# Layer-0 modulation by column blocks: ScalarE and VectorE copies, TensorE products, three projection tiles at once

## The chip, the core and the metric

The kernel runs on one NeuronCore of a Trainium2 chip. The metric is the device time of one execution in microseconds (us), first instruction to last, with the small overhead around it. The engines are TensorE (PE; its weight loads are shown as PEld), VectorE (DVE), ScalarE (ACT), GpSimd (POOL) and SyncE (SP), whose queue starts nearly all transfers. The profile also gives the clock granted to TensorE, as a share of 2.4 GHz; its two levels are 1.2 and 2.4 GHz (0.50 and 1.00).

## The reference

A network of several mixer layers in float32 on 1024 tokens of width 1024. Only the entry of the first layer matters here:

```python
c_act = jax.nn.silu(c)
mod = c_act @ ada_w[layer] + ada_b[layer]            # 1024 -> 3072
shift, scale, gate = jnp.split(mod, 3, axis=-1)
h = rms_norm(x, norm_w[layer]) * (1.0 + scale) + shift
... = even_mixer(h, even_w_in, ...)                   # begins with h @ even_w_in
```

For the first layer, shift and scale are the first 2048 columns of `mod`. They are needed before the first product with `even_w_in`. The gate is needed much later and is computed elsewhere, as before.

## The kernel before

Features lie on the partitions: `X` is eight feature tiles of 128 features by 1024 tokens. Every engine's instructions are written by hand in program order, and engines meet through semaphores only (`signal(...)`, `.up`, `.landed`, `.at`). An engine whose next instruction waits holds back everything behind it, and this is true of SP's queue of transfers too.

**The start.** `sp_start` loads the identity, `x` in two transfers of 2 MB (`XIN`, tokens on partitions), 20 small rows of parameters (`PACKA`, `PACKB`), then the first 2048 columns of `ada_w` as eight blocks of 128 rows (`AWK`, 1 MB each, four buffers). TensorE turns the parameter rows into columns and transposes `x` by feature tiles (`pe_start`, 8 transposes of 128x128 for each tile); ScalarE copies every tile from PSUM to `X` and squares `XIN` for the norm. VectorE multiplies each row block by its entry of silu(c) and adds it up in `ACK` (`dve_row_block`, 2048 columns). When all eight blocks are in, TensorE sums `ACK` over partitions by 16 products with a column of ones (line 598), and VectorE makes `MOD` (shift, scale) and `GS` (the gain). `pe_stay_awake(n, bank)` multiplies the identity n times with a result nobody reads.

**The modulation.** `dve_scaled` multiplies X by the spread reciprocal roots (`XN`); `act_modulate` and `dve_modulate` make `T1 = XN*GS + MOD`, ScalarE rounds it to `HH` and VectorE subtracts to get the rest `HL` (`n_low`), one feature tile after another.

**The projection.** `EVEN_PROJ` is a list of output tiles j = 0, 1, 2, ... of 128 columns of `even_w_in`. A tile's weights are loaded to `WR` by `sp_weights`, rounded to `WH` by ScalarE (`act_high`), and the rest goes to `WL` by GpSimd (`pool_low`). There are two sets of these buffers, for even and odd tiles. `pe_feature` issues six matmuls of 128x512 for one feature k of a tile (WH with HH, WH with HL, WL with HH, each on two halves of the tokens). Tiles 0 and 1 run side by side (`pe_two_tiles`), since they must keep pace with the making of `HL`. Tile 2 and the others follow one by one. Tiles 0 to 2 are the latents; each is copied and squared by ScalarE (`act_latent`) and its squares are summed by TensorE with eight products of one column (`pe_latent_sums`, line 818). Tile 3 is `EVEN_V`, tile 4 `EVEN_KR` (32 columns, `stacked`: four matmuls a feature).

**SP's order around it.** After the row blocks come the weights of tiles 0, 1 and 2 (tile 2's when `WL` of tile 0 is made), the spill of `X`, then, once `n_low` of the last feature is there, five tables for the rotations (COSA, SINA, BLK, COSB, SINB), and only then the weights of tile 3:

```python
for j, t in enumerate(EVEN_PROJ):
    if 0 < j < len(EVEN_PROJ) - 2:
        sp_weights(t + 2)
    if j == 0:
        sp.wait_ge(*ack_summed.at(1))
        sp.wait_ge(*n_low.at(0, DT - 1))
        ... tables ...
```

Of the kernel before, what the change touches and what calls it, by code (L numbers as in the profile page):

```python
# [122 lines left out]
def build(nc, d, where, known):  # L123
# [81 lines left out]

    def places(t):
# [9 lines left out]
    w_loaded = [signal("w_loaded0"), signal("w_loaded1")]  # L216
    w_high, w_low, w_used = signal("w_high"), signal("w_low"), signal("w_used")
# [4 lines left out]

    def sp_weights(t):
        if t >= 2:
            sp.wait_ge(*w_low.at(t - 2))
        raw, _, _ = places(t)
        for dst, src in tiles[t].pieces(raw):
            sp.dma_start(dst, src).then_inc(*w_loaded[t % 2].landed(t))

    def act_high(t):  # L230
        raw, high, _ = places(t)
        user = t - 2
        while user >= 0 and tiles[user].own:
            user -= 2
        act.wait_ge(*w_loaded[t % 2].at(t))
# [9 lines left out]
    def pe_feature(t, k, high, low):  # L245
        s, w = t % 2, tiles[t]
        _, wh, wl = places(t)
        if k == 0:
            pe.wait_ge(*w_low.at(t))
            if t >= 2:  # L250
                pe.wait_ge(*evicted(t - 2))
        both = WH[:, s, 0:w.kt, 0:w.out]
        terms = ((both, high), (both, low)) if w.stacked else ((wh, high), (wh, low), (wl, high))
        for n, (wt, x) in enumerate(terms):
            for h in range(2):
                last = pe.matmul(ps[0:w.out, 2 * s + h, :], wt[:, k, :], x[:, k, halves(h)],  # L256
# [30 lines left out]

    def act_evict(t, dst, func=ACT.Copy, scale=1.0):
# [4 lines left out]
    EVEN_LAT = [tile(cols(even_in, E_CQ + i * P)) for i in range(3)]  # L293
# [190 lines left out]
    AWK, ACK = place("AWK", 79.5, [P, 4, 2 * DM]), place("ACK", 145.5, [P, 2 * DM])  # L484
    XN = place("XN", 175.5, [P, DT, SEQ])
    MKW, MKA = place("MKW", 3, [P, 2, DM]), place("MKA", 11, [P, DM])
    PACKA, PACKB = place("PACKA", 143.5, [P, P]), place("PACKB", 144, [P, P])
# [22 lines left out]
    x_in = [signal("x_in0"), signal("x_in1")]  # L510
    awk_loaded = [signal(f"awk_loaded{i}") for i in range(4)]
    act_scaled = signal("act_scaled")
    awk_used, ack_summed, sums_made, xn_made = signal("awk_used"), signal("ack_summed"), signal("sums_made"), signal("xn_made")
    packs_clear, packs_turned, cols_copied, cs_made = (signal("packs_clear"), signal("packs_turned"), signal("cols_copied"),
                                                       signal("cs_made"))
    x_turned, x_copied, x_spilled, x_back = signal("x_turned"), signal("x_copied"), signal("x_spilled"), signal("x_back")
# [46 lines left out]

    def sp_start():
        sp.dma_start(IDENT[:, :], const("ident")).then_inc(*ident_in.landed())
        for i in range(2):
            sp.dma_start(XIN[:, 4 * i:4 * i + 4, :], d["x"][0].rearrange("(t p) n -> p t n", p=P)[:, 4 * i:4 * i + 4, :]).then_inc(
                *x_in[i].landed())
        sp.wait_ge(*packs_clear.at())
        for i, (dst, src) in enumerate(packs):  # L570
            sp.dma_start(dst, src).then_inc(*packs_in.landed(i))
        for k in range(DT):
            if k >= 4:
                sp.wait_ge(*awk_used.at(k - 4))
            sp.dma_start(AWK[:, k % 4, :], d["ada_w"][0, rows(k), 0:2 * DM]).then_inc(*awk_loaded[k % 4].landed(k))

    def pe_start():
        pe.wait_ge(*ident_in.at())
        pe.wait_ge(*packs_in.at(len(packs) - 1))
        pe.transpose(ps[:, 4, 0:P], PACKA[:, :], IDENT[:, :])  # L580
        pe.transpose(ps[:, 4, P:2 * P], PACKB[:, :], IDENT[:, :]).then_inc(*packs_turned.up())
        for i in range(2):
            pe.wait_ge(*x_in[i].at())
        for f in range(DT):
            if f >= 2:
                pe.wait_ge(*x_copied.at(f - 2))
            for t in range(TT):
                last = pe.transpose(pair(2 * (f % 2))[:, rows(t)], XIN[:, t, rows(f)], IDENT[:, :])
            last.then_inc(*x_turned.up(f))
            if f == 3:  # L590
                pe_spread(0)
        pe.wait_ge(*cols_copied.at())
        pe.wait_ge(*x_copied.at(DT - 1))
        pe_stay_awake(10, 0)
        for half in range(2):
            pe.wait_ge(*awk_used.at(DT - 1, half))
            for m in range(8 * half, 8 * half + 8):
                last = pe.matmul(ps[:, 4, m:m + 1], ACK[:, rows(m)], ONEC[:, 0:1], start=True, stop=True)
            last.then_inc(*ack_summed.up(half))
        pe_stay_awake(20, 0)  # L600

    def act_start():
        for t in range(TT):
            act.wait_ge(*x_in[t // 4].at())
            if t >= 2:
                act.wait_ge(*sums_made.at(t - 2))
            act.activation(SQX[:, t % 2, :], XIN[:, t, :], ACT.Square, accum_out=S1[:, t:t + 1]).then_inc(*sums_made.up(t))
            if t == 2:
                act.wait_ge(*cols_copied.at())
                act.activation(CS[:, :], col["c"], ACT.Silu).then_inc(*cs_made.up())  # L610
        act_root(0)
        for f in range(DT):
            act.wait_ge(*x_turned.at(f))
            act.activation(X[:, f, :], pair(2 * (f % 2)), ACT.Copy).then_inc(*x_copied.up(f))

    def dve_row_block(k):

        dve.wait_ge(*awk_loaded[k % 4].at(k))
        if k:
            dve.wait_ge(*awk_used.at(k - 1))  # L620
        w, c = AWK[:, k % 4, :], CS[:, k:k + 1]
        if k == 0:
            dve.tensor_scalar(ACK[:, :], w, c, None, ALU.mult).then_inc(*awk_used.up(k))
        elif k < DT - 1:
# [3039 lines left out]
```

## Time and profile before

| | us |
|---|---|
| runs, median (lowest to highest of 3) | 2331.66 (2328.37 to 2333.32) |
| profiled execution, its time | 2328.58 |
| profiled execution, its span | 2327.3 |
| granted clock over the span | 0.993 |
| TensorE busy | 2258.5, 97% of the span |
| first matmul of the projection | at 53.25 |
| first matmul of tile 3 | at 91.84 |
| first matmul of tile 4 | at 104.57 |

Times of rows count from the start of the span. A row of the timeline gives start, duration, engine, line, operation, output<-input, count, and in brackets the idle time before it with its releaser. A TensorE product in float32 is recorded as two (a transpose as one), so "x16" for a line of 128x1 products is eight instructions. The last matmul of a row is drawn until it has drained, so rows of TensorE overlap a little; pace is read from start to start.

### The profile page before, as it was taken

To read this page: it belongs to the slowest core of one execution; us is meant where nothing else is said; L and a number is where in the kernel's file an instruction comes from. 1 tells how busy PE (TensorE), PEld (TensorE's weight loads), DVE (VectorE), ACT (ScalarE), POOL (GpSimd) and SP (SyncE) were. 2 spreads that over 40 slices of the span, in tenths; PEclk is the share of its full clock that TensorE was granted. 3 is DMA by queue.
4 is the path that set the end of the run, shared out by engine and by line. 5 is a ranking of instruction groups with operands and counts; after the bars stand their busy time and mean duration, and the time that the engine had idled before them with its cause. 6 is when DMAs were issued, how large, how long until landed. Compare 5 with 4: busy or idle time off the path is not lost.

```text
span 2327.3 us, 29639 instructions
## 1 busy us (share of the span) xinstructions
PE 2258.5 (97%) x11342; PEld 1795.0 (77%) x11342; DVE 1410.2 (61%) x1784; ACT 1045.0 (45%) x1644; POOL 985.5 (42%) x674
## 2 busy tenths in 40 slices
PE   5999999999999999999999999999999999999998
PEld 5888755478888888866688677888878888888887
DVE  6256678668885275268845663442876666666665
ACT  5323265488883264357734562222333333333334
POOL 1111188546652138853122121122365555665551
PEclk9999999999999999999999999999999999999999
DMA  8255300010003133220031311132111111111111
GB/s 318 78 154 161 118 1 5 5 34 1 1 1 118 37 130 109 73 73 11 34 103 43 126 37 37 37 118 64 28 54 55 55 55 55 54 46 47 55 55 73
DMA packets 156385, 154.74 MB, mean 66 GB/s; under 512 B 12550, under 2 KB 141620, under 8 KB 154324
## 3 DMA queue, kind: packets, MB, share of 16 engines
q1 hardware_dynamic: 156244, 152.84, 21.1%
q8 instruction: 91, 1.49, 0.3%
q14 instruction: 50, 0.41, 0.1%
HBM read 128.05 MB, written 20.97 MB: 64 GB/s over the span
## 4 chain that ended last, share of the span: by engine, by line
PE 84%; ACT 5%; DVE 4%; issue 3%; POOL 2%; DMA 1%; SPq 0%; ACTq 0%; DVEq 0%; POOLq 0%
PE ps L256 29%; PE ps L3219 15%; PE ps L3236 9%; PE ps L1946 6%; PE ps L1366 3%; PE ps L1377 2%; PE ps L1165 2%; PE ps L2256 2%; PE ps L2239 2%; PE ps L2225 2%; PE ps L1188 2%; PE ps L1175 1%; PE ps L1348 1%; POOL WSL L3136 1%; ACT B_PR L1249 1%
## 5 line engine op out<-in xcount | busy, mean ns | idle before, releaser
L243 POOL TENSOR_TENSOR WL<-WR,WH 128x1024 fp32r<-128x1024 f32 (+2 forms) x71 | 163.9, 2309 | 656.2 <-ACT WH L238 656.0
L256 PE MATMUL ps<-HH,WH 128*128 128x512 f32 (+2 forms) x880 | 279.8, 399 | 0.4 <-issue 0.3
L256 PE MATMUL ps<-HL,WH 128*128 128x512 f32 (+2 forms) x880 | 273.6, 392 | 0.0
L256 PE MATMUL ps<-HH,WL 128*128 128x512 f32 x848 | 263.2, 392 | 0.0
L3449 DVE TENSOR_TENSOR XF<-ps,XF 128x1024 f32<-128x1024 f32 x168 | 201.6, 1220 | 32.5 <-PE ps L3236 25.9
L3219 PE MATMUL ps<-HC,WSH 128*128 128x512 f32 x640 | 197.1, 389 | 0.0
L256 PEld LDWEIGHTS ps<-HL,WH 128*128 128x128 f32 (+2 forms) x880 | 164.0, 186 | 37.7
L256 PEld LDWEIGHTS ps<-HH,WH 128*128 128x128 f32 (+2 forms) x880 | 160.2, 187 | 38.1 <-issue 5.3
L256 PEld LDWEIGHTS ps<-HH,WL 128*128 128x128 f32 x848 | 160.5, 189 | 34.2
L3136 POOL TENSOR_TENSOR WSL<-WSR,WSH 128x512 fp32r<-128x512 f32 x100 | 131.4, 1314 | 107.5 <-ACT WSH L3130 107.5
L3130 ACT ACTIVATE WSH<-WSR 128x512 fp32r<-128x512 f32 x100 | 62.9, 629 | 218.2 <-POOL WSR L3118 218.2
L3118 POOL TENSOR_TENSOR WSR<-WS 128x512 f32<-128x512 f32 x100 | 133.9, 1339 | 34.4 <-PE ps L3219 34.4
L3219 PE MATMUL ps<-HS,WSH 128*128 128x512 f32 x480 | 147.8, 389 | 0.0
L3219 PEld LDWEIGHTS ps<-HC,WSH 128*128 128x128 f32 x640 | 120.1, 188 | 25.0
L3219 PE MATMUL ps<-HC,WSL 128*128 128x512 f32 x320 | 124.5, 389 | 0.0
L3136 POOL TENSOR_TENSOR WSL<-WS,WSH 128x512 fp32r<-128x512 f32 x48 | 64.7, 1352 | 127.5 <-ACT WSH L3130 127.5
L3236 PE MATMUL ps<-AH,OWH 128*128 128x512 f32 x352 | 109.8, 393 | 6.4 <-DVE XF L3449 4.5
L3408 DVE TENSOR_TENSOR CG<-CG,ps 128x512 f32<-128x512 f32 x60 | 41.3, 688 | 119.1 <-ACT CG L3297 89.4
L3236 PE MATMUL ps<-AH,OWL 128*128 128x512 f32 x352 | 108.6, 390 | 0.0
L3236 PE MATMUL ps<-AL,OWH 128*128 128x512 f32 x352 | 108.5, 389 | 0.0
L238 ACT ACTIVATE WH<-WR 128x1024 fp32r<-128x1024 f32 (+2 forms) x73 | 68.5, 939 | 87.4 <-PE ps L256 72.8
L3219 PEld LDWEIGHTS ps<-HS,WSH 128*128 128x128 f32 x480 | 90.1, 188 | 18.7
(460 smaller groups left out, 5309.6 us busy)
## 6 DMA issues: line engine op xcount, KB each, us to landing
WS<-in_w_ffn_in SPq DMA_DIRECT2D x44, 512.0 KB, 5.1
MKW<-in_ada_w SPq DMA_DIRECT2D x32, 512.0 KB, 4.1
spill<-X SPq DMA_DIRECT2D x3, 4096.0 KB, 13.9
OW<-in_w_ffn_out SPq DMA_DIRECT2D x22, 512.0 KB, 3.6
WR<-in_w_in SPq DMA_DIRECT2D x19, 512.0 KB, 3.8
WR<-in_even_w_in SPq DMA_DIRECT2D x17, 512.0 KB, 4.1
AWK<-in_ada_w SPq DMA_DIRECT2D x8, 1024.0 KB, 9.3
X<-spill SPq DMA_DIRECT2D x2, 4096.0 KB, 13.6
```

The source lines that it names most:

```text
L238: act.activation(high[:, :, :], raw[:, :, :], ACT.Copy).then_inc(*w_high.up(t))
L243: pool.tensor_tensor(low[:, :, :], raw[:, :, :], high[:, :, :].bitcast(F32), ALU.subtract).then_inc(*w_low.up(t))
L256: last = pe.matmul(ps[0:w.out, 2 * s + h, :], wt[:, k, :], x[:, k, halves(h)], start=(k == 0 and n == 0), stop=(k == w.kt - 1 and n == len ...
L1165: last = pe.matmul(ps[:, b + j, :], qs[:, rows(q)], ks[:, halves(j)], start=(n == 0), stop=(n == len(passes) - 1))
L1366: last = pe.matmul(ps[:, e, :], keys[:, rows(k)], q[:, halves(u % 2)], start=(n == 0), stop=shifted)
L1946: last = pe.matmul(ps[:, bank, :], w[q % ORING][:, k, :], x[:, k, :], start=(k == 0 and m == 0), stop=(k == DT // 2 - 1 and m == 2))
L3118: pool.tensor_tensor(WSR[:, q % RING, :, :], w_block(*a), w_block(*b), op).then_inc(*ws_sum.up(q))
L3130: act.activation(WSH[:, q % RING, :, :], src, ACT.Copy).then_inc(*ws_high.up(q))
L3136: pool.tensor_tensor(WSL[:, q % RING, :, :], src, WSH[:, q % RING, :, :].bitcast(F32), ALU.subtract).then_inc(*ws_low.up(q))
L3219: last = pe.matmul(ps[:, BANK[o], :], w[:, q % RING, k, :], OPERAND[o][:, x, k, :], start=(k == 0 and n == 0), stop=(k == HK - 1 and n == 2))
L3236: done = pe.matmul(ps[:, 4 + 2 * (n % 2) + h, :], w[:, rows(n)], x[:, halves(h)], start=(first and m == 0), stop=(last and m == 2))
L3449: dve.tensor_tensor(LAST.x[:, n, :], pair(4 + 2 * (n % 2)), LAST.x[:, n, :], ALU.add).then_inc(*y_added.up(r, n))
```

## The change

It rewrites the start and the first three projection tiles.

- `x` comes in four transfers. Only `PACKA` is turned at the start; `PACKB` is loaded later and turned within the projection (`pe_packs`).
- `ada_w` comes by blocks of columns, `sp_mod_columns(f)`: for feature tile f, 128 shift and 128 scale columns of all 1024 rows (`AWC`, two transfers of 512 KB, four buffers). The block f needs the place of the block f-4.
- `pe_mod_columns(f)` makes shift and scale of feature tile f by 2 x 8 products of 128x1 with `CS` = silu(c), accumulated in PSUM. `BY_PE` is 8, so this holds for all eight tiles; `dve_mod_sum`, the way over VectorE, is issued for none.
- VectorE copies six of the eight tiles of X from PSUM, ScalarE two. The spread roots are copied to `RCS`. One VectorE instruction makes `T1 = X*GS*RCS`, ScalarE adds the shift while rounding to `HH`, and VectorE's `dve_lower` makes `HL`; `XN` is gone.
- `pe_three_tiles` runs tiles 0, 1 and 2 side by side; tile 2 has its own buffers (`LAT_THIRD`) and PSUM banks 4 and 5. Before feature k it issues the products for tile k+2.
- The sums of all three latents come after tile 3.
- SP waits for the end of tile 2 (`w_used`) before the tables, since BLK lies where tile 2's rest weights are.

```diff
+    def pe_three_tiles(high, low, made, before):
+        ts = range(3)
+        for k in range(DT - 1):
+            before(k)
+            pe.wait_ge(*made(k))
+            for t in ts:
+                pe_feature(t, k, high, low)
+        before(DT - 1)
+        pe.wait_ge(*made(DT - 1))
+        for t in (1, 0, 2):
+            pe_feature(t, DT - 1, high, low)
...
+    BY_PE, BY_ACT = 8, (3, 5)
...
+    def sp_mod_columns(f):
+        if f < 4:
+            sp.wait_ge(*awk_loaded[f].at("x", f))
+        else:
+            sp.wait_ge(*ack_summed.at(f - 4))
+        for part in range(2):
+            src = d["ada_w"][0, :, part * DM + f * P:part * DM + (f + 1) * P].rearrange("(k p) n -> p k n", p=P)
+            sp.dma_start(AWC[:, f % 4, :, rows(part)], src).then_inc(*awk_loaded[f % 4].landed(f, part))
...
+            for part in range(2):
+                for k in range(DT):
+                    last = pe.matmul(ps[:, 6 + f % 2, 2 * f + part:2 * f + part + 1], AWC[:, f % 4, k, rows(part)], CS[:, k:k + 1],
+                                     start=(k == 0), stop=(k == DT - 1))
...
     def pe_start():
         pe.wait_ge(*ident_in.at())
+        pe_start_turn(0)
+        pe_start_turn(1)
+        pe.wait_ge(*packs_in.at(len(rows_a) - 1))
+        pe.transpose(ps[:, 6, 0:P], PACKA[:, :], IDENT[:, :]).then_inc(*packs_turned.up("a"))
+        for f in range(2, 5):
+            pe_start_turn(f)
+        pe.wait_ge(*cols_copied.at("a"))
+        pe_spread(0, spot=RC_SPOT)
+        for f in range(5, DT):
+            pe_start_turn(f)
+        for f in range(DT):
+            pe.wait_ge(*x_copied(f))
+        pe_mod_columns(0)
+        pe_stay_awake(10, 0)
+        pe_mod_columns(1)
+        pe_stay_awake(10, 0)
...
+        dve.scalar_tensor_tensor(T1[:, f % 2, :], X[:, f, :], GS[:, 0, f:f + 1], RCS[:, :], ALU.mult, ALU.mult).then_inc(
+            *n_scaled.up(0, f))
...
             if j == 0:
-                sp.wait_ge(*ack_summed.at(1))
                 sp.wait_ge(*n_low.at(0, DT - 1))
+                sp.wait_ge(*w_used.at(2))
                 for i, (dst, n) in enumerate(((COSA, "cosA"), (SINA, "sinA"), (BLK, "blk64"), (COSB, "cosB"), (SINB, "sinB"))):
...
-        pe_two_tiles(EVEN_PROJ[0], EVEN_PROJ[1], HH, HL, lambda k: n_low.at(0, k))
+        def before(k):
+            for f in {0: (2,), DT - 1: ()}.get(k, (k + 2,)):
+                if f < DT:
+                    pe_mod_columns(f)
+            if k == DT - 1:
+                pe_packs()
+
+        pe_three_tiles(HH, HL, lambda k: n_low.at(0, k), before)
         for j, t in enumerate(EVEN_PROJ):
-            if j > 1:
+            if j > 2:
                 pe_tile(t, HH, HL, beside=lambda k: beside(j, k))
-            if 1 <= j < 4:
-                pe_latent_sums(j - 1)
+            if j == 3:
+                pe.wait_ge(*ev_act.at(EVEN_LAT[2]))
+                for c in range(3):
+                    pe_latent_sums(c)
...
     def act_even_proj():
-        act_two_tiles(EVEN_PROJ[0])
         act_modulate()
         act.wait_ge(*qk_gains.at())
+        act_high(3)
+        act.wait_ge(*x_spilled.at(0))
+        for c in (1, 0, 2):
+            act_latent(c)
```

**SP's queue between the spill of X and the weights of tile 4** (`spill`, the five tables, then `WR` of tile 3 and of tile 4), before:

```order
L744 DMA spill<-X 128x8192 [waits x_copied]
L752 DMA COSA<-in_consts 128x1024 [waits n_low,ack_summed]
L752 DMA SINA<-in_consts 128x1024
L752 DMA BLK<-in_consts 128x128
L752 DMA COSB<-in_consts 128x1024
L752 DMA SINB<-in_consts 128x1024
L228 DMA WR<-in_even_w_in 128x8x128 [waits w_low]
L228 DMA WR<-in_even_w_in 128x8x32 [waits w_low]
```

The same place in SP's queue after the change:

```order
L817 DMA spill<-X 128x8192 [waits x_copied_dve,x_copied_act]
L825 DMA COSA<-in_consts 128x1024 [waits w_used,n_low]
L825 DMA SINA<-in_consts 128x1024
L825 DMA BLK<-in_consts 128x128
L825 DMA COSB<-in_consts 128x1024
L825 DMA SINB<-in_consts 128x1024
L235 DMA WR<-in_even_w_in 128x8x128 [waits w_low]
L235 DMA WR<-in_even_w_in 128x8x32 [waits w_low]
```

The order is the same; the first table now waits for `w_used`, which tile 2's last matmul raises, and the tables and both weight loads stand behind it.

**TensorE at the start of the projection**, before (`n_low` is HL of a feature made; the products of line 598 give shift and scale of all tiles):

```order
L598 MATMUL ps<-ONEC,ACK 128x1 [waits awk_used]
L598 MATMUL ps<-ONEC,ACK 128x1 x7
L374 MATMUL ps<-IDENT 128x128 x20
L256 MATMUL ps<-HH,WH 128x512 [waits w_low,n_low]
L256 MATMUL ps<-HH,WH 128x512
L256 MATMUL ps<-HL,WH 128x512 x2
L256 MATMUL ps<-HH,WL 128x512 x2
L256 MATMUL ps<-HH,WH 128x512 [waits w_low]
```

TensorE after the change, from tile 2's part of feature 0 (its weights are in `LAT_THIRD`) to the first matmuls of feature 1:

```order
L263 MATMUL ps<-HH,LAT_THIRD_88 128x512 [waits w_low]
L263 MATMUL ps<-HH,LAT_THIRD_88 128x512
L263 MATMUL ps<-HL,LAT_THIRD_88 128x512 x2
L263 MATMUL ps<-HH,LAT_THIRD_89 128x512 x2
L645 MATMUL ps<-CS,AWC 128x1 [waits awk_loaded3,mod_made]
L645 MATMUL ps<-CS,AWC 128x1 x15
L263 MATMUL ps<-HH,WH 128x512 [waits n_low]
L263 MATMUL ps<-HH,WH 128x512
```

A block of 16 products of 128x1 now stands ahead of each of the features 0 to 5, each followed by 18 matmuls of 128x512.

## Rows read from the trace of the kernel before

**Rows 1.** The page: span, busy time of engines, and the chain's shares.
```profile
span 2327.3 us, 29639 instructions
PE 2258.5 (97%) x11342; PEld 1795.0 (77%) x11342; DVE 1410.2 (61%) x1784; ACT 1045.0 (45%) x1644; POOL 985.5 (42%) x674
PE 84%; ACT 5%; DVE 4%; issue 3%; POOL 2%; DMA 1%; SPq 0%; ACTq 0%; DVEq 0%; POOLq 0%
```
**Rows 2.** The chain in order of time, 0 to 160 us: start, duration, what.
```profile
39.09 4.58 DVE ACK L629 x2
43.72 3.30 PE ps L598 x16
47.02 6.47 PE ps L374 x40
53.49 19.07 PE ps L256 x84
...
90.16 1.68 PE ps L818 x16
91.84 11.05 PE ps L256 x48
102.89 1.68 PE ps L818 x16
104.57 7.42 PE ps L256 x32
```
**Rows 3.** Line 567, the two transfers of x: starts, and time to landing.
```profile
L567 SPq DMA_DIRECT2D XIN<-in_x x2: 423/465/507, 1.2 to 1.7; - x2
DMA to landing us min/median/max: 8.0/10.4/12.8
```
**Rows 4.** The timeline of TensorE, 14 to 56 us.
```profile
17.56 0.45 PE L580 MATMUL ps<-IDENT,PACKA 128*128 128x128 f32 x1 [17.56 <-DMA PACKB<-in_a_k_norm]
...
18.01 3.62 PE L588 MATMUL ps<-IDENT,XIN 128*128 128x128 f32 x16
...
30.06 1.20 PE L406 MATMUL ps<-IDENT,SQX 128*128 128x128 f32 x8
31.10 1.91 PE L588 MATMUL ps<-IDENT,XIN 128*128 128x128 f32 x16
...
36.47 2.47 PE L374 MATMUL ps<-IDENT 128*128 128x128 f32 x20 [1.21 <-ACT X L614]
```
**Rows 5.** Groups by line and form, 0 to 400 us: busy, mean ns, idle.
```profile
L988 DVE COPY VA<-ps 128x1024 f32<-128x1024 f32 x1 | 1.2, 1225 | 0.8 <-PE ps L865 0.8
```
**Rows 6.** Stretches: busy of each engine, PEclk (third from the end), DMA, GB/s.
```profile
40.00:45.00 5.00, 3.23 (x24) 3.15 (x24) 4.80 (x3) 0.84 (x1) 5.00 (x2) 0.90 0.18 32
45.00:50.00 5.00, 5.00 (x24) 5.00 (x25) 2.46 (x5) 2.50 (x3) 0.88 (x1) 0.50 1.16 466
50.00:55.00 5.00, 5.00 (x36) 4.71 (x35) 5.00 (x5) 3.05 (x3) 0.00 (x0) 0.91 1.02 439
...
75.00:80.00 5.00, 4.66 (x26) 3.89 (x25) 0.00 (x0) 3.33 (x4) 2.78 (x2) 0.82 0.22 41
80.00:85.00 5.00, 5.00 (x20) 4.06 (x19) 0.00 (x0) 0.00 (x0) 0.76 (x1) 0.84 0.39 105
...
1460.00:1465.00 5.00, 5.00 (x23) 4.62 (x22) 0.00 (x0) 0.00 (x0) 0.00 (x0) 0.56 0.00 0
1465.00:1470.00 5.00, 5.00 (x18) 4.02 (x17) 1.16 (x2) 0.00 (x0) 0.00 (x0) 0.76 0.00 0
```
**Rows 7.** The timeline of TensorE, 1450 to 1472 us.
```profile
1457.63 1.92 PE L2648 MATMUL ps<-ONEC,OS 128*128 128x1 f32 x16 [0.60 <-DVE MIX L2899]
1459.41 0.71 PE L256 MATMUL ps<-HH,WH 128*128 128x512 f32 x2
...
1461.13 3.41 PE L2648 MATMUL ps<-ONEC,OS 128*128 128x1 f32 x16
```
**Rows 8.** The timeline, 66 to 112 us: tables, and tile 3's weights.
```profile
66.42 0.34 SPq L752 DMA_DIRECT2D COSA<-in_consts  x1
...
68.71 39.06 SPq L228 DMA_DIRECT2D WR<-in_even_w_in  x5
...
77.25 1.08 ACT L238 ACTIVATE WH<-WR 128x1024 fp32r<-128x1024 f32 x1
78.40 2.36 POOL L243 TENSOR_TENSOR WL<-WR,WH 128x1024 fp32r<-128x1024 f32 x1 [2.22 <-ACT WH L238]
```
**Rows 9.** Transfers issued 66 to 70 us: count, size, us to landing.
```profile
WR<-in_even_w_in SPq DMA_DIRECT2D x1, 512.0 KB, 7.4
```

More of the change, by code:

```diff
@@ L255, in pe_feature @@
             for h in range(2):
-                last = pe.matmul(ps[0:w.out, 2 * s + h, :], wt[:, k, :], x[:, k, halves(h)],
+                last = pe.matmul(ps[0:w.out, bank_of(t) + h, :], wt[:, k, :], x[:, k, halves(h)],
                                  start=(k == 0 and n == 0), stop=(k == w.kt - 1 and n == len(terms) - 1))
@@ L292, in build @@
     even_in, odd_in, second_in = d["even_w_in"][0], d["odd_w_in"][0], d["w_in_2"][0]
-    EVEN_LAT = [tile(cols(even_in, E_CQ + i * P)) for i in range(3)]
+    LAT_THIRD = own_places("LAT_THIRD", 35, 39, 43)
+    EVEN_LAT = [tile(cols(even_in, E_CQ + i * P), own=LAT_THIRD if i == 2 else None) for i in range(3)]
     EVEN_V = tile(cols(even_in, E_V))
@@ L564, in sp_start @@
     def sp_start():
         sp.dma_start(IDENT[:, :], const("ident")).then_inc(*ident_in.landed())
[L566 to L575, printed above, removed]
+        for i in range(4):
+            sp.dma_start(XIN[:, 2 * i:2 * i + 2, :], d["x"][0].rearrange("(t p) n -> p t n", p=P)[:, 2 * i:2 * i + 2, :]).then_inc(
+                *awk_loaded[i].landed("x", i))
@@ new lines, in sp_start, with pe_start_turn @@
+        sp.wait_ge(*packs_clear.at("a"))
+        sp_pack(0)
+        for t in range(3):
+            sp_weights(t)
+            sp_mod_columns(t)
+        sp_mod_columns(3)
+        sp.wait_ge(*packs_clear.at("b"))
+        sp_pack(1)
+        for f in range(4, DT):
+            sp_mod_columns(f)
+    def pe_start_turn(f):
+        if f >= 3:
+            pe.wait_ge(*x_copied(f - 3))
+        for t in range(TT):
+            if f == 0 and t % 2 == 0:
+                pe.wait_ge(*awk_loaded[t // 2].at("x", t // 2))
+            last = pe.transpose(pair(2 * (f % 3))[:, rows(t)], XIN[:, t, rows(f)], IDENT[:, :])
+        last.then_inc(*x_turned.up(f))
@@ new lines, in pe_mod_columns @@
+    def pe_mod_columns(f):
+        if f >= 2:
+            pe.wait_ge(*mod_made.at(0, "sum", f - 2))
+        if f >= BY_PE:
+            pe.wait_ge(*awk_used.at(f, DT - 1))
+            for part in range(2):
+                last = pe.matmul(ps[:, 6 + f % 2, 2 * f + part:2 * f + part + 1], ACK[:, f % 2, rows(part)], ONEC[:, 0:1], start=True,
+                                 stop=True)
+        else:
+            if f == 0:
+                pe.wait_ge(*cs_made.at())
+                pe.wait_ge(*rcs_made.at())
+            pe.wait_ge(*awk_loaded[f % 4].at(f, 1))
+            for part in range(2):
+                for k in range(DT):
+                    last = pe.matmul(ps[:, 6 + f % 2, 2 * f + part:2 * f + part + 1], AWC[:, f % 4, k, rows(part)], CS[:, k:k + 1],
+                                     start=(k == 0), stop=(k == DT - 1))
+        last.then_inc(*ack_summed.up(f))
@@ L577, in pe_start @@
     def pe_start():
         pe.wait_ge(*ident_in.at())
-        pe.wait_ge(*packs_in.at(len(packs) - 1))
[L580 to L600, printed above, removed]
+        pe_start_turn(0)
+        pe_start_turn(1)
+        pe.wait_ge(*packs_in.at(len(rows_a) - 1))
@@ new lines, in pe_start, with pe_packs @@
+        pe.transpose(ps[:, 6, 0:P], PACKA[:, :], IDENT[:, :]).then_inc(*packs_turned.up("a"))
[11 more added lines that the diff above has]
+        pe_stay_awake(10, 0)
+    def pe_packs():
+        pe.wait_ge(*mod_made.at(0, "sum", DT - 1))
+        pe.wait_ge(*packs_in.at(len(packs) - 1))
+        pe.transpose(ps[:, 7, 0:P], PACKB[:, :], IDENT[:, :]).then_inc(*packs_turned.up("b"))
@@ L661, in dve_start @@
[L661 to L680 removed]
+        dve_lower(0)
@@ L739, in sp_even_proj @@
     def sp_even_proj():
-        sp_weights(EVEN_PROJ[0])
-        sp_weights(EVEN_PROJ[1])
-        sp_weights(EVEN_PROJ[2])
-        sp.wait_ge(*x_copied.at(DT - 1))
+        for f in range(DT):
+            sp.wait_ge(*x_copied(f))
         sp.dma_start(d["spill"], X[:, :, :]).then_inc(*x_spilled.landed(0))
```

191 lines of the change are left out of this document (99 added, 92 removed).

## The prediction

> **What bounds the kernel now.** I read the page first: TensorE is busy 97% of the span of 2327.3 us and carries 84% of the chain that ended last [rows 1]. So a change to the start is worth what it moves TensorE's later work, and little behind it can give time back. Next, the chain in order of time [rows 2]. From 39.09 it runs over the last row block on VectorE (ending 43.7), the sums of 128x1 on TensorE, then the stay-awake matmuls into the first projection matmul at 53.5. From there on it is TensorE: tiles 0, 1, 2, one set of latent sums at 90.16, tile 3 at 91.84, a second set at 102.89, tile 4 at 104.57. I take the start of tile 4 as the mark, because from there both kernels issue the same work in the same order, and ask where the mark lies after the change.
>
> **When the start is over (PE free for the first block).** Its second half of x is issued at 1.7 and lands 12.8 later, so at 14.5 [rows 3]; four transfers bring the same bytes, so I keep 14.5 for the last. Tile 0 then lacks two transposes, tile 1 has eight. Sixteen took 3.4 us (3.62 with the drain) when TensorE had been idle, 0.21 each [rows 4]: 0.4 + 1.7 gives 16.6. PACKA stands behind x as the small rows did before, whose last landed at 17.4 to 17.5 [rows 4]. It may come as early as x, 14.5, but I take 17.4, the row it is nearest to. Turned at 17.6. Tiles 2, 3, 4 at 1.7 each: 22.7. The eight spread transposes ran in 1.04 start to start: 23.9 with its waits. Tiles 5, 6, 7 at the later pace of 0.12 each [rows 4], under 1.0 each: 26.7. VectorE copies tiles 6 and 7 from PSUM at 1.22 each, by a copy of this form [rows 5]: 28.4, and `pe_mod_columns(0)` waits for that. Bounds: 26 with early parameters, 31 if all transposes keep the slow pace. ScalarE's squares, roots and copies and the ada blocks of 1 MB lie beside this. The first of these blocks is issued right behind x, with one weight tile ahead of it, so it is there long before 28.4.
>
> The Trainium skill bears on the bound of 31: "TensorE: Matmul & The Clock Gate", Part 4 (PE-mode transpose), says that transposes do not count as work that raises the clock. The row at 31.10 speaks against it: 16 transposes in 1.91 us after the same took 3.62, with nothing but transposes between. By the page the sum would end about 3 us later, by the row where I put it.
>
> **The blocks of products (added).** The trace has no block of 16, but it has the same form in eights: weights of 128x128, one column. Eight took 1.68, so 0.21 each [rows 2], and 3.30 at the lower clock, 0.41 each [rows 2]. A block is 16, so 3.36 us at 2.4 GHz and 6.6 at 1.2. Eight blocks are 26.9 us of TensorE. Removed with them: the 16 sums of line 598 and 10 of the 30 stay-awakes, as well as VectorE's row blocks, all of them ahead of the old mark of 53.5 and already absent from the line above. Two blocks and two runs of ten stay-awakes (2.3 each without drain [rows 4]) come first: 28.4 + 6.7 + 4.6 = 39.7.
>
> **Three tiles with six blocks.** Tile 3 took 11.05 for 48 matmuls [rows 2], 1.38 for one feature. Three tiles are 24 x 1.38 = 33.1; the six blocks 20.2; PACKB's transpose 0.2. TensorE is never waited out by VectorE here: a feature costs TensorE 7.5 us, VectorE two instructions of about 1.2 and two of 0.2. End of the three tiles at a full clock: 93.2. Before, three tiles and one set of sums ended at 91.8.
>
> **The clock (added).** After eight products of one column the rows show the clock fall in places: from 78.2 to 81.6 (PEclk 0.82 in 75 to 80 and 0.84 in 80 to 85), 44 to 50.9 with sums of one column and a short idle at its start, and again near 1460 [rows 6]. That last place is the nearest to the new pattern: eight products, then six dense matmuls in 1.7 us, then eight products, which run at half pace, 3.41 us [rows 7], and some 6.4 us at 1.2 GHz in all (0.56 of one stretch, 0.76 of the next [rows 6]). The eights at 90.16 and 102.89, without idle before them and dense work on both sides, kept their pace of 1.68. The new blocks are twice that long and without a pause between products. So I expect a fall at each of the eight. A fall costs half its length: 1.7 us for one of 3.4, up to 3.3 for one of 6.4 to 6.9. Bounds are 0 (as at 90.16) and 8 x 3.3 = 26. I take eight short ones, 14, since every block from the third on is followed by 4.1 us of dense matmuls. End of the three tiles: 107.
>
> **Tile 3's weights (a wait moved).** SP now holds the tables, and behind them tile 3's weights, until tile 2's last matmul. Before, this load was issued at 68.7, when tile 1 was still running, and used at 91.8, so it never showed. Now all of it does: 2.3 us from the first table's issue to the load's [rows 8], 7.4 until it lands behind 2 MB of tables [rows 9], 1.06 for WH on ScalarE, 2.36 for WL on GpSimd [rows 8], some 0.2 between. That is 13.3 us in which TensorE has nothing; tile 1's eviction is 2 us on ScalarE and done inside it. Behind the wait on SP stand tile 4's weights too, on ScalarE the latents' copies; both are ready before tile 3 ends. Tile 3 starts at 120.3 and runs 11.05 plus what the clock costs after so long an idle. The nearest place is around 45 to 50, some 6.9 us at 1.2 GHz (0.90 of the stretch before and 0.91 of the one after [rows 6]), so 1.7 to 3.4. I take 2.5: 133.9. Then three sets of latent sums, 5.0, of which the second and third stood at 90.16 and 102.89 before: mark at 138.9.
>
> **The sum.** 138.9 - 104.6 = 34.3 us later. The profiled execution was 2328.58 us, which gives 2363; the median of the runs is 3.1 above that profile, so 2366.
>
> **The rivals.**
> 1. The clock stays up through the blocks, as through the eights at 90.16 and 102.89. Then 14 us fall away: +20, 2352. For it: those two rows. Against it: blocks twice as long, and the place near 1460.
> 2. The clock is low for most of the phase: blocks at 0.41 a product and falls of 6.4 us or more, 26 in place of 14, and another fall after the three sets of sums, 1.7. +48, 2380. For it: near 1460 one fall covered two sets and what lay between.
> 3. Faster. One mechanism: the weight loads of the one-column products slip under the matmuls in flight, so a block costs next to nothing and the clock does not fall. Without 26.9 and 14 the sum is -6.6, 2325. It decides at about 0.8 us a block, 0.05 a product, where even with the wait for tile 3 the two kernels are level. Against it: 0.21 in every undisturbed row of the form, under and after dense work alike. The Trainium skill's table in "TensorE: Matmul & The Clock Gate", Back-to-back issue gap, gives about 25 ns for matmuls of 1 to 64 columns, which for two passes of 16 would be 0.8 us a block. Its LDWEIGHTS section gives the number of columns divided by 1.2, 107 ns a load and 3.4 us a block, and the rows agree with that one.
> 4. The wait for tile 3's weights doesn't show, because the load is not held as I read the queue, and the clock stays up: +20 - 13.3 - 2.5 = +4, 2336.
>
> **How the numbers follow.** Forecast 0.55 (2357 to 2373), rival 1 0.20 (2346 to 2357), rival 2 0.20 (2373 to 2388), rival 3 0.02, rival 4 0.03. The start's bounds (-2.4, +2.6) are inside each case's own range. Range 2348 to 2379: it leaves out the small cases, the lower end of rival 1 and the upper half of rival 2. Differences under 0.2%, about 5 us, are what a measurement of this kernel cannot tell from none. Faster 0.02 (rival 3), same 0.03 (rival 4), slower 0.95 (the rest).
>
> **What would show each step.** The first 128x1 product of line 645 starts near 28. Blocks last 3.4 us where PEclk is 1.0 and up to 6.6 where it is 0.5. PEclk between 30 and 107 lies near 0.8; at 1.0 throughout rival 1 holds, under 0.7 rival 2. Between the last matmul of LAT_THIRD and the next of WH lies an idle of about 13 us whose chain reads: wait for the weights' transfer, WH on ScalarE, WL on GpSimd. Tile 4 starts near 139, and from there the traces run parallel. The forecast is wrong if that idle is under 5 us, if a block costs under 2 us, or if later stretches give back more than a few us.

## The result

| | before | after |
|---|---|---|
| runs, median (range) | 2330.93 us (2328.37 to 2333.32, 4 runs) | 2372.70 us (2368.49 to 2375.92, 4 runs) |
| ratio, 95% interval | | 1.0178 (1.0156 to 1.0200) |
| profiled execution: span | 2327.3 | 2374.6 |
| granted clock over the span | 0.993 | 0.979 |
| first matmul of the projection | 53.25 | 49.63 |
| first matmul of tile 4 | 104.57 | 148.09 |

The changed kernel is 41.8 us slower by the medians. The profiled execution is the slowest of its four, with the lowest granted clock of them (0.979; the others 0.981 to 0.983), and 47.3 us slower by the spans, so the terms below add up to 47.

The page of the kernel after, its answer to [rows 1]:

```profile
span 2374.6 us, 30061 instructions
PE 2305.5 (97%) x11546; PEld 1836.8 (77%) x11546; DVE 1394.3 (59%) x1791; ACT 1037.9 (44%) x1636; POOL 984.1 (41%) x674
PE 86%; ACT 5%; DVE 3%; issue 3%; DMA 2%; POOL 1%; SPq 1%; ACTq 0%; DVEq 0%; POOLq 0%
```

VectorE lost 16 us of work and TensorE, which carries the chain, gained 47 us of busy time. The chain in order of time, 0 to 200 us (start, duration, what), the answer to [rows 2]:

```profile
26.32 4.14 PE ps L645 x32
30.46 4.48 PE ps L395 x20
34.94 6.62 PE ps L645 x32
41.55 4.47 PE ps L395 x20
46.03 3.74 PE ps L645 x32
49.77 5.83 PE ps L263 x18
55.60 3.46 PE ps L645 x32
59.07 5.82 PE ps L263 x18
64.89 4.62 PE ps L645 x32
69.51 6.28 PE ps L263 x18
...
99.45 8.33 PE ps L263 x36
107.78 0.11 PE ps L671
107.89 4.14 PE ps L263 x18
...
114.51 8.11 DMA WR<-in_even_w_in
...
122.70 1.06 ACT WH L245
...
123.83 2.35 POOL WL L250
...
126.22 13.79 PE ps L263 x48
140.01 8.07 PE ps L891 x48
148.09 9.42 PE ps L263 x32
```

Line 645 is a block of 16 products, line 395 ten stay-awakes, line 263 the dense matmuls. At full speed a block takes 3.46 and 18 dense matmuls 4.14; most rows here are longer. Behind the last of them come 14.2 us in which TensorE stands, for the reason that the rows name: the transfer of tile 3's weights, their rounding on ScalarE, their rest on GpSimd. The granted clock (third number from the end) of stretches:

```profile
25.00:46.00 21.00, 19.68 (x106) 19.72 (x106) 5.40 (x9) 4.19 (x4) 4.02 (x3) 0.60 0.81 212
46.00:70.00 24.00, 24.00 (x135) 21.52 (x134) 5.98 (x11) 2.30 (x2) 1.82 (x1) 0.78 0.61 212
70.00:90.00 20.00, 20.00 (x102) 17.46 (x101) 5.63 (x9) 2.30 (x2) 0.00 (x0) 0.76 0.16 68
```

TensorE was busy for the whole of the second and third stretch, and yet had the lower clock for nearly half of them.

After the mark at tile 4 the difference is 43.5 us. Tile 4 itself runs partly at 1.2 GHz (9.42 instead of 7.42, +2.0), and a set of sums near 292 us, after 2.91 us of idle as before, now runs at the lower level (3.55 instead of 1.95, +1.6). That is the rest of the 47.3.

### The profile page after: what moved, and what is told of

It is laid out like the page before. It is cut to its first block, busy times and chain, and to the rows that moved or that the text cites. A ratio compares the mean times of both kernels' runs of the same rounds, so it can differ in the third digit from the quotient of the medians.

```text
span 2374.6 us, 30061 instructions
## 1 busy us (share of the span) xinstructions
PE 2305.5 (97%) x11546; PEld 1836.8 (77%) x11546; DVE 1394.3 (59%) x1791; ACT 1037.9 (44%) x1636; POOL 984.1 (41%) x674
## 4 chain that ended last, share of the span: by engine, by line
PE 86%; ACT 5%; DVE 3%; issue 3%; DMA 2%; POOL 1%; SPq 1%; ACTq 0%; DVEq 0%; POOLq 0%
PE ps L263 30%; PE ps L3300 16%; PE ps L3317 10%; PE ps L2027 6%; PE ps L1447 2%; PE ps L1458 2%; PE ps L1246 2%; PE ps L2337 2%; PE ps L2320 2%; PE ps L2306 2%; PE ps L1269 2%; PE ps L645 1%; PE ps L1256 1%; PE ps L1429 1%; ACT B_PR L1330 1%
## 5 line engine op out<-in xcount | busy, mean ns | idle before, releaser
L250 POOL TENSOR_TENSOR WL<-WR,WH 128x1024 fp32r<-128x1024 f32 (+1 forms) x70 | 160.6, 2294 | 703.6 <-ACT WH L245 703.5
L263 PE MATMUL ps<-HH,WH 128*128 128x512 f32 (+2 forms) x864 | 281.0, 407 | 14.6 <-POOL WL L250 14.2
```

Of the source, the lines that this page charges most:

```text
L250: pool.tensor_tensor(low[:, :, :], raw[:, :, :], high[:, :, :].bitcast(F32), ALU.subtract).then_inc(*w_low.up(t))
L263: last = pe.matmul(ps[0:w.out, bank_of(t) + h, :], wt[:, k, :], x[:, k, halves(h)], start=(k == 0 and n == 0), stop=(k == w.kt - 1 and n = ...
```

## The experiments

All are compared with the changed kernel (2372.7) and the kernel before (2330 to 2332 in each set of runs). PEclk is the granted clock. "Dense matmuls" are those of 128x512 of the projection, a "product" is one of a single column. Lines and rows are those of one profiled execution of each version.

### Tile 3's weights issued ahead of the tables

```diff
-            if 0 < j < len(EVEN_PROJ) - 2:
+            if 1 < j < len(EVEN_PROJ) - 2:
                 sp_weights(t + 2)
             if j == 0:
+                sp_weights(3)
                 sp.wait_ge(*n_low.at(0, DT - 1))
                 sp.wait_ge(*w_used.at(2))
```

> The changed kernel with one edit: SP issues the weights of tile 3 before it waits for the end of tile 2, and only then the five tables. Nothing else moves. My theory (14.2 us of idle and 2.9 us of half speed in tile 3 are the held load): the idle before tile 3 falls to what rounding and splitting its weights take after tile 1's last matmul, 3.6 us less the 2.8 us that tiles 0 and 2 still run, so about 0.8 us, and tile 3 keeps its pace: 16 us faster than the changed kernel, 2356. Rival (the idle is ScalarE and GpSimd work and a busy transfer engine, not the place in the queue): under 5 us faster.

Measured: 2353.94 us, ratio to the kernel before 1.0099 (1.0081 to 1.0117). That is 18.8 us less than the changed kernel. The chain:

```profile
101.78 1.40 PE ps L263 x6
...
103.28 1.07 ACT WH L245
...
104.42 2.39 POOL WL L250
...
106.85 11.17 PE ps L263 x48
118.03 5.87 PE ps L892 x48
123.89 9.97 PE ps L263 x32
```

The transfer is gone from the chain, the idle is 0.95 us and tile 3 keeps its pace, 11.17. So the place in SP's queue was the cause. Of the 18.8 us, 13.3 are idle, 2.6 the pace of tile 3 and 2.2 that of the sums (5.87 instead of 8.07), by the two profiled executions.

These two differ in one more place. TensorE's instructions up to the end of the three tiles are the same in both, and yet that end came at 105.9 here and at 112.0 in the changed kernel's. The clock fell in other places: here the 18 dense matmuls behind a block took 6.61 us at first, then 4.25 in some features and 5.85 in others, there 5.82 to 6.50 in each of the first five.

### Four tiles by VectorE

```diff
-    BY_PE, BY_ACT = 8, (3, 5)
+    BY_PE, BY_ACT = 4, (3, 5)
```

> The changed kernel with BY_PE = 4 in place of 8: the modulation of feature tiles 4 to 7 is multiplied and added up by VectorE (eight instructions of 128x256 each) and TensorE only sums the partitions, two products of one column for each tile in place of sixteen. My theory (each block of 16 costs TensorE 3.5 us and a fall of the clock of about 2): 4 blocks and their falls go, about 21 us, and VectorE, which then needs some 6.2 us for a feature where TensorE needs 4.6, gives 2 to 4 back: 17 us faster than the changed kernel, 2355. Rival (VectorE's row of 32 dependent instructions becomes the bound of the projection): within 5 us of the changed kernel or slower.

Measured: 2354.19 us, 1.0098 (1.0083 to 1.0113), 18.5 less than with all eight on TensorE. VectorE, where it is the bound (start, duration, engine, line, operation):

```profile
58.44 0.35 DVE L710 TENSOR_SCALAR ACK<-AWC,CS 128x256 f32<-128x256 f32 x1
58.82 3.61 DVE L707 SCALAR_TENSOR_TENSOR ACK<-AWC,CS,ACK 128x256 f32<-128x256 f32 x7
62.34 0.15 DVE L733 TENSOR_TENSOR MOD<-ps,COLA 128x2 f32<-128x2 f32 x1
```

One tile's sum takes 4.0 us and a feature 6.7 of VectorE's time, and the chain runs through it from 57 to 78 us. Still the four blocks were dearer on TensorE: giving it all eight tiles instead of the first four costs 18.5 of the 41.8 us.

### The same products, one behind each dense matmul

```diff
                 last = pe.matmul(ps[0:w.out, bank_of(t) + h, :], wt[:, k, :], x[:, k, halves(h)],
                                  start=(k == 0 and n == 0), stop=(k == w.kt - 1 and n == len(terms) - 1))
+                for product in next(among, ()):
+                    product()
...
             before(k)
             pe.wait_ge(*made(k))
-            for t in ts:
-                pe_feature(t, k, high, low)
+            products = pe_mod_products(k + 2) if k + 2 < DT else []
+            slots = [products[i:i + 1] for i in range(len(products))] + [[]] * 18
+            for i, t in enumerate(ts):
+                pe_feature(t, k, high, low, among=slots[6 * i:6 * i + 6])
...
+            dve_lower(f - 1)
             dve_scaled(f)
-            dve_lower(f - 1)
```

> The changed kernel with the same 96 products of feature tiles 2 to 7, but one behind each matmul of the feature before instead of sixteen in a row (and VectorE makes the rest of feature f-1 before it scales feature f, so that it does not wait for the later sums). Same instructions, same data. My theory (the rows of 16 products of one column make the clock fall): granted clock 1.0 from the first dense matmul to the end of the three tiles, which saves the 12 us between 46 and 112 us that the clock took there: 2361. Rival (the clock falls by the total of the products, or of an idle array, however they lie): same time as the changed kernel, clock near 0.8 there. Second rival (weight loads no longer hide under dense matmuls): 96 x 0.1 = 10 us slower at a full clock.

Measured: 2359.66 us, 1.0125 (1.0108 to 1.0142), 13.0 less than in rows of sixteen. The edit also changes the order of VectorE's work and of TensorE's waits, as the diff shows; TensorE has no idle for VectorE between 46 and 90 us in either kernel. Its stretches, granted clock third from the end:

```profile
46.00:70.00 24.00, 24.00 (x157) 21.70 (x156) 8.67 (x12) 3.45 (x3) 0.00 (x0) 1.00 0.67 238
70.00:90.00 20.00, 20.00 (x128) 17.96 (x127) 7.21 (x11) 2.30 (x2) 0.00 (x0) 1.00 0.08 32
```

The records of TensorE in feature 0 (start, time, engine, line, operation):

```profile
43.82 0.48 PE L264 MATMUL ps<-HL,WH 128*128 128x512 f32 x1
44.14 0.28 PE L661 MATMUL ps<-CS,AWC 128*128 128x1 f32 x2
44.28 0.47 PE L264 MATMUL ps<-HH,WL 128*128 128x512 f32 x1
```

A pair takes 0.46 from start to start, what the two cost apart (0.23 and 0.21), so neither the products nor their weight loads are dearer. Only the clock differs: 1.00 for 0.77. That shows that here the rows of products, and not their number, make it fall. From the start of the third block or first pair to the end of the three tiles it is 54.7 us instead of 66.0.

### Two products in place of sixteen

```diff
-                for k in range(DT):
+                for k in range(DT if f < 2 else 1):
...
-                                     start=(k == 0), stop=(k == DT - 1))
+                                     start=(k == 0), stop=(k == (DT if f < 2 else 1) - 1))
```

> The changed kernel with two products in place of sixteen for each of feature tiles 2 to 7 (it leaves out seven eighths of their modulation's sum), the loads and waits unchanged. It measures what the six blocks cost with all that hangs on them. My theory: 6 x 14/16 x 3.46 = 18 us of the products and 12 us of half speed, 30 us faster, 2342, with the clock near 1.0 between 50 and 85 us. Rival (the clock falls for the transposes and stay-awakes of the start, not for the blocks): 18 us faster, 2354, and PEclk still near 0.8.

Measured (this kernel leaves out seven eighths of the sums for tiles 2 to 7): 2342.78 us, 1.0049 (1.0034 to 1.0064), 29.9 less. A feature takes 4.59 us throughout (4.25 and 0.34 in the chain), PEclk is 1.00 from 46 to 70. This is the whole price of 14/16 of the six blocks: 18 us are the 84 products left out at 0.21 each, and the 12 that remain I put down to the clock. They agree with the 13.0 of the spread kernel, in which the products are as many as in the changed one.

### Latent sums apart

On top of the early load, the three sets of eight sums stand behind features 3, 5 and 7 of tile 3.

```diff
+            if j == 3 and k in (3, 5, 7):
+                if k == 3:
+                    pe.wait_ge(*ev_act.at(EVEN_LAT[2]))
+                pe_latent_sums((k - 3) // 2)
...
-                for c in range(3):
-                    pe_latent_sums(c)
```

> As the kernel with tile 3's weights issued early, and the three sets of latent sums (8 products of one column each) stand apart inside tile 3, after its features 3, 5 and 7, instead of 24 products in a row behind it. Same instructions. My theory (rows of one-column products longer than eight make the clock fall, eights between dense work don't): tile 3 with its sums and tile 4 keep full pace, which the early-weights kernel did not (5.9 us for the sums instead of 5.0, 10.0 for tile 4 instead of 7.4): 3.4 us less than it, 2350.5, clock 1.00 from the end of the three tiles on. Rival: the same total of products gives the same fall, 2354.

Measured: 2353.59 us, 1.0096 (1.0080 to 1.0112), against 2353.94 with the sums in a row. In its place the theory holds:

```profile
115.48 1.68 PE ps L892 x16
117.16 2.89 PE ps L263 x12
120.05 1.68 PE ps L892 x16
121.72 2.89 PE ps L263 x12
124.61 1.68 PE ps L892 x16
126.29 7.42 PE ps L263 x32
```

Every set takes 1.68 and tile 4 its full pace, 7.42 instead of 9.97. From the start of tile 3 to the end of tile 4 this execution took 24.0 us and the one above 27.0. But its three tiles ended 2.9 us later (108.8), with the same instructions of TensorE before them: the third block took 6.62 us and the dense matmuls behind it 6.63. So in the time of the whole kernel the gain is not shown.

### The three gains together, all eight tiles by TensorE

> All eight feature tiles still multiplied by TensorE; the products of tiles 2 to 7 one behind each matmul, tile 3's weights issued early, the latent sums apart inside tile 3: three measured gains together. If they add up (-13 from the spreading, -19 from the early load, -3 from the sums, each in its own stretch of the span): end of the three tiles near 97.4 as in the spread kernel, tile 4 at 114, ten us behind the kernel before: 2340. If the clock's loss is only moved (a rival), the sum of the three gains is not reached: 2348 or more.

Measured: 2342.96 us, 1.0053 (1.0037 to 1.0069). They add up within 3 us: tile 4 starts at 114.87. With every stall and every later fall removed, the all-TensorE start is still some 11 us behind the kernel before. The profiled execution starts its dense matmuls 10.8 us earlier than the kernel before (42.71 for 53.49 in the chain) and takes 21.1 us longer from there to tile 4 (72.2 for 51.1). Of these, 20.2 are the 96 products of 0.21 us that now stand in the projection, so what is left is the bare price of that work on TensorE.

### A mixed version without stay-awakes

VectorE multiplies tiles 1, 4 and 6, TensorE the rest; blocks 0 and 2 in a row before the projection; no stay-awakes.

> A version meant to beat both. As the one before, but VectorE multiplies the modulation of tiles 1, 4 and 6 (4.0 us each, in its idle time), TensorE that of 0, 2, 3, 5 and 7; products of tile k+3 stand among the matmuls of feature k; no stay-awake matmuls; ScalarE rounds the weights of tiles 1 and 2 before the first HH. First dense matmul at 35 instead of 49.6, three tiles 45 us, end at 80, tile 4 at 97 to 99 against 104.6 before: 2323 to 2326, 5 to 8 us faster than the kernel before. Rival (VectorE, with 36 us of work between 26 and 75 us, holds back HL): tile 4 at 104 or later, no faster than before.

Measured: 2339.34 us, 1.0032 (1.0018 to 1.0045). Slower than the kernel before and 15 us over the forecast. The first dense matmul came at 41.5, since VectorE's sum of tile 1 ended at 33.8 and TensorE, at 1.2 GHz, needed 6.8 us for the block behind it. What I had not expected came then. The clock of 35 to 46 was 0.50, and that of 46 to 70 was 0.66: feature 0, in which a product stood behind each matmul, ran from 41.5 to 56 all at 1.2 GHz, with pairs of 0.85 us. The spreading that had kept the clock up did not bring it up.

### Without the stay-awakes

```diff
         pe_mod_columns(0)
-        pe_stay_awake(10, 0)
         pe_mod_columns(1)
-        pe_stay_awake(10, 0)
```

> The changed kernel without the two runs of ten stay-awake matmuls behind blocks 0 and 1. Theory: nothing that TensorE needs comes in that time, so the first dense matmul moves from 49.6 to about 42, as soon as HL of feature 0 is made, and the clock, already low after blocks of one-column products, loses at most one more fall: 6 to 9 us faster than the changed kernel, 2365. Rival (they keep the clock up and are worth their time, or VectorE's chain to HL sets the start anyway): within 2 us of it.

Measured: 2366.54 us, 1.0140 (1.0120 to 1.0160); runs from 2356.4 to 2368.6. 6.2 us faster than the changed kernel, at the lower edge of what was expected. Three blocks ran in a row from 26.0 to 43.7, and the first dense matmuls at 1.2 GHz (7.05 for 18).

### Spread products without the stay-awakes

The same edit on the spread kernel, to see what the clock does when the alternation starts low.

> The spread kernel (products one behind each matmul, 2359.7) without the two runs of stay-awake matmuls, nothing else. It asks what the clock does when the alternating pattern starts at 1.2 GHz. Theory A (the pattern keeps the level at which it starts: at 1.2 GHz half of its time is one-column work): PEclk 0.5 over most of features 0 to 5, 46 us at full speed becoming 70 or more, so 10 to 20 us slower than the spread kernel. Theory B (the level depends on the pattern alone, and the low start of the mixed version had to do with what stood before it): one fall at the start, then 1.0, some 6 us faster, 2353.

Measured: 2400.85 us, 1.0302 (1.0289 to 1.0315). 41.2 us slower than the spread kernel, from 20 stay-awakes taken away. Its stretches:

```profile
50.00:60.00 10.00, 10.00 (x36) 8.83 (x35) 1.60 (x3) 0.99 (x1) 0.00 (x0) 0.50 0.14 40
60.00:70.00 10.00, 10.00 (x37) 8.85 (x36) 1.28 (x1) 0.16 (x1) 0.00 (x0) 0.50 0.25 66
...
110.00:120.00 10.00, 10.00 (x35) 8.75 (x36) 2.89 (x4) 1.15 (x1) 0.00 (x0) 0.50 0.00 0
```

The records of TensorE in one of these stretches (start, time, engine, line, operation):

```profile
60.54 0.77 PE L264 MATMUL ps<-HL,WH 128*128 128x512 f32 x1
61.11 0.42 PE L661 MATMUL ps<-CS,AWC 128*128 128x1 f32 x2
61.39 0.77 PE L264 MATMUL ps<-HH,WL 128*128 128x512 f32 x1
```

All six features with products ran at 0.50, each 14.5 us long instead of 7.7, and the clock rose only in features 6 and 7, which have none. Theory A holds and by more than I gave it. The same instructions in the same order keep 2.4 GHz for 46 us or 1.2 GHz for more than 80, by the level at which they start; the four runs of each version lie within 6 us of each other (2358 to 2364, 2397 to 2403), so this is not one odd execution.

### Two more versions meant to beat both

The first alternates: VectorE multiplies tiles 1, 3, 5, 7, and both runs of stay-awakes stay.

> A second version meant to beat both, on the ground of the all-TensorE one with the three gains (2343): VectorE multiplies tiles 1, 3, 5 and 7 (each 4.0 us of its time, between the rest of feature f-1 and the scaling of feature f), TensorE 0, 2, 4 and 6; both runs of ten stay-awakes are kept, because the mixed version without them ran its whole feature 0 at 1.2 GHz. Theory: first dense matmul at 38.5 instead of 42.7; features that carry 16 products 7.7 us, the others 4.6; end of the three tiles at 84, tile 4 at 101: 3 us faster than the kernel before, 2328, if the clock is 1.0 when the first dense matmul starts. Rival: it starts at 1.2 GHz again and keeps it while products and matmuls alternate: feature 0 takes 14 us, no faster than before (2335 or more).

Measured: 2333.85 us, 1.0011 (0.9997 to 1.0025): level with the kernel before, twelve runs from 2326 to 2341. The profiled one is the slowest of them. Its records of TensorE:

```profile
42.35 0.47 PE L264 MATMUL ps<-HH,WH 128*128 128x512 f32 x1 [2.03 <-DVE HL L768]
...
43.70 0.48 PE L264 MATMUL ps<-HL,WH 128*128 128x512 f32 x1
...
44.16 0.75 PE L264 MATMUL ps<-HH,WL 128*128 128x512 f32 x1
```

The dense matmuls began at 42.35 at full speed, after 2 us of idle, the clock fell at 44, among the first pairs, and PEclk was 0.50 from 46 to 60. Feature 0 took 13.0 us, near the 14 of the rival, but not for the reason that it gives, since the pattern had begun at 2.4 GHz. So to begin at the higher level was not enough here; one thing that differs from the spread kernel, which has stay-awakes up to its first dense matmul, is the idle before. From 62.7 on, where a dense stretch had brought the clock back to 1.00, the next features with products kept it. The other runs have no trace, but their granted clocks are on record: the five of 2326 to 2330 us had 0.993 or 0.994, the other seven (2332 to 2341) 0.988 to 0.990. So the scatter goes with the clock.

The second keeps products out of feature 0.

> As the alternate version, but no products stand in feature 0: TensorE starts the projection with 18 dense matmuls, so that the clock is up before products and matmuls alternate. VectorE multiplies tiles 1, 2, 4, 6; feature 1 carries the products of tiles 2 and 3, features 2 to 5 those of 4 to 7; one run of ten stay-awakes, behind the sums of tile 1. Theory (the alternating pattern keeps the level at which it starts, a dense stretch lifts it): PEclk back at 1.0 by the end of feature 0 at the latest and 1.0 from there, features 1, 3, 5 in 7.7 to 8.3 us; end of the three tiles near 86, tile 4 at 103: 2329, one to three us faster than the kernel before, and less scatter between runs than the alternate version (2326 to 2341). Rival: the level in features 1 to 5 is chance, the runs scatter as before and some lie above 2338.

Measured: 2338.31 us, 1.0028 (1.0017 to 1.0040), runs from 2334 to 2343, six of the twelve above 2338. The forecast of 2329 failed:

```profile
46.93 0.77 PE L264 MATMUL ps<-HH,WH 128*128 128x512 f32 x1 [2.18 <-issue]
47.49 0.42 PE L660 MATMUL ps<-ONEC,ACK 128*128 128x1 f32 x2
```

Feature 0 began early, at 37.55, and at full speed, but it was broken by waits: 0.58 and 1.64 us for the rest weights of tiles 1 and 2, then 2.18 us before feature 1, where TensorE waits for VectorE's sum of tile 2 (its last instruction ends at 46.83). The alternation then ran at 1.2 GHz from its first matmul (0.77 us each), and the level held until past 60. That is no proof of the rival, which calls the level chance. As in the version above, TensorE had stood for some 2 us just before the clock fell; no run here has the dense stretch without the waits, so that it would help then is not shown.

### The kernel before, with two edits

```diff
-        pe_stay_awake(20, 0)
+        pe_stay_awake(14, 0)
...
+            if (j, k) == (2, 3):
+                pe_latent_sums(0)
...
-            if 1 <= j < 4:
+            if 2 <= j < 4:
                 pe_latent_sums(j - 1)
```

> The kernel before, with what the runs showed of the clock applied in two places and nothing of the change: 14 stay-awakes instead of 20 behind the sums of the row blocks (HL of feature 0 was there at 51.1, TensorE came at 53.25), and the first set of latent sums moved from between tiles 1 and 2 into tile 2, behind its feature 3, among dense matmuls. Theory: start 2 us earlier, and the fall from 78.2 to 81.6 (1.7 us) goes: 3 to 4 us faster than the kernel before, 2327. Rival (the idle before tile 2 of some 0.7 us makes the clock fall just the same, and fewer stay-awakes leave it low into the first matmuls): within 1 us.

Measured: 2328.97 us, 0.9986 (0.9977 to 0.9995), against 2331.79 for the kernel before in the same set, 2.8 us faster. One half of it worked in the profiled execution (2332.85 us, the slowest of the eleven):

```profile
76.06 5.74 PE ps L256 x24
81.80 1.68 PE ps L818 x16
83.48 5.61 PE ps L256 x24
```

The fall from 78.2 to 81.6 in [rows 6] is gone. Fewer stay-awakes gave nothing there, since the fourteen ran wholly at 1.2 GHz, 5.75 us for what was 6.47 with twenty, and the projection started at 53.05. Tile 4 came 1.1 us earlier than before (103.49). Where the other runs gained the rest of the 2.8 us has no trace here. It is the one version that beats both kernels, by little.

## Why the prediction was right, and where it was off

The forecast was 2366 (2348 to 2379), the median 2372.7, by the mechanisms it named. Part of the nearness is luck: the forecast added 3.1 us for a median above the profiled execution, and here the profiled execution lies 3.2 above the median. Between the profiled executions it had 34.3 us and 47.3 were measured. By its steps, on the profiled execution:

- **Start.** The first block was put at 28.4 and came at 26.3: PACKA was turned at 16.5, not 17.6, and tiles 2, 3 and 4 took 3.97 us for their 24 transposes instead of 5.1. The last part of x landed at 14.3, taken as 14.5.
- **Blocks.** 3.46 each at full speed, forecast 3.36; 6.62 at the lower level, forecast 6.6. Eights of the same form were the right row.
- **Clock.** Its size is the largest miss of this execution. Blocks 0 to 7 took 33.9 us instead of 8 x 3.46 = 27.7 (6.2), the two runs of stay-awakes 8.95 instead of 4.6 (4.4), the dense matmuls 42.7 instead of 33.1 (9.6). Together 20 instead of 14. I had counted one short fall for a block and half-speed dense work behind it. But blocks and stay-awakes themselves were caught at 1.2 GHz too. From 30 to 46 PEclk was 0.50 throughout. From 30 to 107 it was 0.74, where the forecast said near 0.8. End of the three tiles: 112.0, forecast 107. But the size is not a fixed one: the same instructions of TensorE lost 13.8 us to the clock in the execution with early weights (26.58 to 105.92, at full speed 65.5) and 17.1 in the one with the sums apart, so the 14 lies at the low end of what the runs show. The mechanism was right, and the spread kernel and the one with two products show it apart from the work.
- **Tile 3's weights.** 14.2 us of idle, forecast 13.3; the transfer took 8.1 instead of 7.4. Loss of pace in tile 3: 2.7, forecast 2.5.
- **Sums and tile 4.** Three sets in a row were priced at 5.0 and took 8.07, and tile 4 lost 2.0. I had put that fall into rival 2 alone, though it is the same cause as the blocks': 24 one-column products in a row, half as many again as a block. The version with the sums apart shows it: no fall, 1.68 a set. The mark came at 148.1, forecast 138.9. Of the nine us, 5 arose at the three tiles, 1 at the idle, 3 here. Behind the mark the traces were to run parallel; tile 4's lost 2.0 and the 1.6 near 292 us say otherwise.
- **Rivals.** The clock did not stay up (rival 1); PEclk was 0.78 and 0.76 from 46 to 90, and the clock's 20 us lie halfway between the forecast's 14 and rival 2's 26. Rival 3 fell with the blocks' 3.46. Rival 4 fell with the idle, and the experiment with the early load shows the wait to be just what the queue's order says.

Without the wait, 23 us of the loss remain. Without the falls of the clock from the projection on as well, 11 remain (the version with the three gains), and those are the products themselves, less what the earlier start gives back.

## What to carry to other kernels

Rows of one-column matmuls can make TensorE's clock fall though the engine is busy all the time: blocks of 16 between dense matmuls gave PEclk 0.78 and 0.76 from 46 to 90 us, a row of 24 behind tile 3 cost the sums and tile 4 five us, while sets of eight inside tile 3 kept their 1.68. Where the falls come differs from one execution to the next, so judge such a change by several runs and not by one trace. Put the products one by one behind dense matmuls, and see that the clock is up, and TensorE has not just stood idle, when that pattern begins. When three steps become one longer one, look at each queue for the transfers that were behind the end of the first; here one line's place in SP's queue cost 19 us.

## What the runs showed of the hardware that was not expected

- The alternation of one 128x512 matmul and one 128x1 product held either level: 46 us at 1.00 with pairs of 0.46 us, or over 80 us at 0.50 with pairs of 0.85. Twenty matmuls of 128x128 ahead of it decided 41 us. The higher level is not safe in it: after 2 us of idle it fell 1.8 us into the pattern (the first of the two versions meant to beat both). Why the lower level did not rise by itself is open. The Trainium skill, in "TensorE: Matmul & The Clock Gate" (Why this matters for your kernels), asks for TensorE to be kept busy and free of idle gaps to stay at the higher level. The trace agrees for idle: after the 14.2 us before tile 3 the first matmuls ran at 1.2 GHz and the tile lost 2.7 us. It goes beyond it: in the alternation the engine had no gap and stayed low.
- Transposes of 128x128 changed their pace with nothing else on TensorE: in the changed kernel's start 0.21 us each at first and 0.11 from the spread on, and in [rows 4] likewise. The stay-awakes, also of 128x128, have the same two paces, 0.22 a record at PEclk 0.50 and 0.12 at 1.00, so I take it for the clock, lifted by transposes. The granted clock of the profile doesn't confirm this: it reads 1.00 from the start of the span on, at the slow pace too. Part 4 (PE-mode transpose) of the Trainium skill's page "TensorE: Matmul & The Clock Gate" says that the full clock doesn't engage for transposes; these paces speak against it for transposes in float32.
- In the version with four tiles by VectorE, eight dependent VectorE instructions of 128x256 take 4.0 us: 0.35 for the first, which reads one tensor, and 0.51 each for the other seven, which read two, the second being the result of the one before. Which of the two makes the difference is not shown.
